# Attention stage of a diffusion trunk: maxima of 512, 256, 768 and 1024 columns, two buffers of turned probabilities, squares in PSUM, roots ahead of the last copy

## The chip, the core and the metric

The kernel runs on one core of one Trainium2 chip. TensorE multiplies matrices into PSUM, VectorE (DVE) and ScalarE (ACT) work elementwise and reduce, GpSimd (POOL) and SyncE (SP) issue transfers. The engines run side by side, each in the order of its own instructions, and wait for one another by semaphores. The metric is the device time of one execution in microseconds; lower is better.

## The reference

One layer of a hybrid trunk over 1024 latent tokens with 256 context tokens ahead of them: differential attention, a convolution branch and a gated delta network, merged, then a mixture of experts. The change lies in the attention alone:

```
def diff_softmax_attend(q, k, v, lam):
    s = jnp.einsum("bhmqd,bhmkd->bhmqk", q, k, preferred_element_type=jnp.float32) * (A_HEAD_DIM ** -0.5)
    p = jax.nn.softmax(s, axis=-1)
    a = p[:, :, 0] - lam * p[:, :, 1]
    return jnp.einsum("bhqk,bhkd->bhqd", a.astype(v.dtype), v)

    def finish(o):
        return (rms_norm(o, subln_w, SUBLN_EPS) * (1.0 - lambda_init)).reshape(o.shape[0], o.shape[1], A_WIDTH)
```

There are 4 heads, each with two maps m of 64 dimensions, 1024 queries in blocks of 128, 1280 keys (256 context, 1024 latent), and values of 128 dimensions. All is fp32.

## The kernel before

The stages run one after the other with a barrier between them; `attend` is one, `branches` follows it. `attend` treats 32 heads of query blocks, numbered j = 4 x block + head. TOK is 1280, P is 128, N is 32, NKT is 10.

For each j these steps are taken. **Scores** (L806, TensorE): six matmuls put both maps' 128 x 1280 scores into the five PSUM banks of `p_scores`; map 0 lies in columns 0 to 1279, map 1 in 1280 to 2559. Their order is map 1 columns 0 to 255, map 0 0 to 511, map 1 256 to 767, map 0 1024 to 1279 ("scored_tails"), map 0 512 to 1023 ("scored0"), map 1 768 to 1279 ("scored1"); the two maps use different halves of the array's rows and run side by side. **Maxima** (L941 to L954, VectorE): the reductions below give each row's maximum of each map, and two "bounds" (L946) turn them into the exponentials' bias `minus_max`. **Exponentials** (L885, ScalarE): one per map over 1280 columns, with the sum. **Sums and mix** (L967, L968, L974, VectorE): the ratio of the sums, and p0 + ratio x p1 into `p0`. **Turn** (L821, TensorE): ten transposes in three groups, of 4, 4 and 2, into two PSUM buffers `p_turned`. **Store** (L872, ScalarE): the three groups are copied to `aT` in SBUF. **Weigh** (L830, TensorE): ten matmuls of `aT` with the values into `p_out`. **Save** (L898, L899, ScalarE): the sum of the squares of the output, with the squares themselves written to `o_squares`, which nobody reads, and the scaled output to `o_raw`. **Root** (L905, ScalarE), for a batch of 8 heads or 4, five times (after heads 7, 15, 23, 27 and 31): the square root needs another function table than the exponential, so a table is loaded (ACT_TABLE_LOAD) ahead of it and another ahead of the next exponential. **Norm** (L982, L983, VectorE) divides, and L840 and L910 turn and store the finished outputs of a block, in eight of the steps.

The order on each engine is written by hand and software-pipelined. In iteration j TensorE runs scores of j+1, turn of j-2's last group, (finished outputs,) weigh of j-2, turn of j-1's first two groups. ScalarE runs store of j-2's groups 0 and 1, save of j-3, store of j-2's group 2, (finished outputs, root,) exponentials of j+1. VectorE runs sums of j, maxima of j+1, mix of j, (norm). The scores of j+1 wait for both exponentials of j ("exped"), as `p_scores` is one buffer. On VectorE each reduction waits for the one before it (`ch.run` is an instruction and the wait for its own end), and `after(eng, name, j, ...)` waits for step j's signal.

## Time and profile before

| | us |
|---|---|
| median of 3 runs | 2865.71 (2860.67 to 2866.39) |
| the profiled execution, its own time | 2864.54 |
| its span in the trace | 2862.7 |
| attention: first scores start | 958.49 |
| attention: last output copy starts | 1213.12 |

Over the whole span TensorE is busy 90%, VectorE 44%, ScalarE 20%. These are averages over stages with different limits. Attention is about 9% of the span, and what a change in it is worth is read from its own steps: a repeating pattern of instructions on three engines, in which the end of one engine's wait is another's work. In a row of the trace in order of time the first number is the start in us from the span's start, the second the duration; a bracket tells how long the engine sat idle before it and who released it. The matmul rows of one block are merged, with their count.

### The profile page before, as it was taken

To read this page: it belongs to the slowest core of one execution; us is meant where nothing else is said; L and a number is where in the kernel's file an instruction comes from. 1 tells how busy PE (TensorE), PEld (TensorE's weight loads), DVE (VectorE), ACT (ScalarE), POOL (GpSimd) and SP (SyncE) were. 2 spreads that over 40 slices of the span, in tenths; PEclk is the share of its full clock that TensorE was granted. 3 is DMA by queue.
4 is the path that set the end of the run, shared out by engine and by line. 5 is a ranking of instruction groups with operands and counts; after the bars stand their busy time and mean duration, and the time that the engine had idled before them with its cause. 6 is when DMAs were issued, how large, how long until landed. Compare 5 with 4: busy or idle time off the path is not lost. (4 is left out here: it accounts for less than half of the span.)

```text
span 2862.7 us, 57067 instructions
## 1 busy us (share of the span) xinstructions
PE 2588.4 (90%) x23169; PEld 1366.0 (48%) x23169; DVE 1261.7 (44%) x2179; ACT 568.6 (20%) x1080; POOL 474.1 (17%) x711
## 2 busy tenths in 40 slices
PE   5999858888898788799999999999499999999995
PEld 3444447776444466644444444445244444333442
DVE  2466656664764488504884211125422222222221
ACT  4333222322221377600000110013100000000000
POOL 0011145552111000000000000000023332233222
PEclk7999968999999999999999999999699999999998
DMA  6011010000010000030222231112677899869532
GB/s 236 22 30 36 1 47 11 19 19 31 22 44 0 15 1 1 1 81 26 81 74 77 73 100 59 34 52 95 236 295 268 336 377 400 331 226 352 202 85 77
DMA packets 198512, 320.17 MB, mean 112 GB/s; under 512 B 13601, under 2 KB 135944, under 8 KB 198120
## 3 DMA queue, kind: packets, MB, share of 16 engines
q1 hardware_dynamic: 183175, 294.11, 28.3%
q0 software_dynamic: 15168, 23.60, 3.7%
q8 instruction: 132, 2.16, 0.3%
q14 instruction: 37, 0.30, 0.0%
HBM read 299.63 MB, written 22.50 MB: 113 GB/s over the span
## 5 line engine op out<-in xcount | busy, mean ns | idle before, releaser
L2697 PE MATMUL p_gate_up<-w_unit,rowsT 128*32 128x512 f32 x4672 | 521.7, 597 | 17.6 <-DVEq L2739 8.1
L2034 PE MATMUL p_gate<-hT,w_gate 128*128 128x512 f32 x768 | 341.9, 598 | 6.5 <-DVE region L2158 5.3
L2697 PEld LDWEIGHTS p_gate_up<-w_unit,rowsT 128*32 128x32 f32 x4672 | 162.9, 111 | 331.1 <-issue 304.5
L2711 PE MATMUL p_y<-w_unit,hiddenT 128*32 128x256 f32 x4672 | 268.0, 381 | 1.2 <-DVE hiddenT L2753 1.2
L1080 PE MATMUL p_w<-hT,w_c 128*128 128x512 f32 (+1 forms) x640 | 248.7, 550 | 0.0
L2583 DVE STREAM_TRANSPOSE rows_turned<-rows 128x256 f32<-128x256 f32 x74 | 33.0, 445 | 452.3 <-PE p_gate_up L2697 447.5
L2034 PEld LDWEIGHTS p_gate<-hT,w_gate 128*128 128x128 f32 x768 | 144.0, 191 | 182.3 <-issue 180.7
L2711 PEld LDWEIGHTS p_y<-w_unit,hiddenT 128*32 128x32 f32 x4672 | 163.2, 111 | 123.7 <-issue 44.6
L1080 PEld LDWEIGHTS p_w<-hT,w_c 128*128 128x128 f32 x640 | 121.5, 190 | 124.9 <-issue 121.6
L2734 ACT ACTIVATE sigmoid<-p_gate_up 128x256 f32<-128x256 f32 x73 | 28.2, 386 | 746.0 <-PE p_gate_up L2697 746.0
L2183 DVE SCALAR_TENSOR_TENSOR region<-gated,taps,region x120 | 154.1, 1284 | 16.0
L2664 POOL DMA_INDIRECT sum_rows<-y,rows_to_add x73 | 117.6, 1611 | 150.7 <-DVE y L2761 144.0
L1996 POOL DMA_DIRECT2D half_region<-in_w_out x1 | 1.1, 1102 | 814.8 <-PE p_branch L2039 814.8
L2158 DVE TENSOR_TENSOR product<-p_branch,gate 128x512 f32<-128x512 f32 x32 | 22.1, 691 | 226.9 <-PE p_branch L2039 226.3
L941 DVE TENSOR_REDUCE part_max<-p_scores 128x1 f32<-128x512 f32 (+2 forms) x128 | 105.6, 825 | 36.2 <-PE p_scores L806 30.4
L806 PE MATMUL p_scores<-region 64*128 64x512 f32 (+1 forms) x384 | 84.3, 575 | 26.3 <-ACT p L885 24.8
L2098 ACT ACTIVATE gate<-p_gate 128x512 f32<-128x512 f32 x48 | 28.6, 596 | 358.4 <-PE p_gate L2034 358.4
L830 PE MATMUL p_out<-region,aT 128*128 128x128 f32 x640 | 80.9, 282 | 13.0 <-ACT aT L872 12.7
L885 ACT ACTIVATE p<-p_scores,minus_max 128x1280 f32<-128x1280 f32 x64 | 84.9, 1327 | 26.3 <-DVE minus_max L946 25.8
L1221 DVE SCALAR_TENSOR_TENSOR conv<-raw,head_taps,conv 128x1284 f32<-128x1284 f32 (+1 forms) x48 | 89.0, 1854 | 1.7
L674 DVE RECIPROCAL rinv<-root 128x512 f32<-128x512 f32 (+1 forms) x20 | 60.5, 3025 | 63.2 <-ACT root L609 63.2
L2574 POOL DMA_INDIRECT rows<-xn_rows,rows_to_gather x75 | 74.8, 997 | 62.7 <-POOL rows_to_gather L2652 60.1
(368 smaller groups left out, 3528.3 us busy)
## 6 DMA issues: line engine op xcount, KB each, us to landing
w_unit<-in_w_gate SPq DMA_DIRECT2D x128, 512.0 KB, 14.9
w_unit<-in_w_up SPq DMA_DIRECT2D x128, 512.0 KB, 16.5
w_unit<-in_w_down SPq DMA_DIRECT2D x128, 512.0 KB, 11.7
w_b<-in_w_mod SPq DMA_DIRECT2D x32, 512.0 KB, 3.9
w_gate<-in_w_in SPq DMA_DIRECT2D x24, 512.0 KB
region<-in_w_mod SPq DMA_DIRECT2D x4, 2048.0 KB, 14.7
w_c<-in_w_in SPq DMA_DIRECT2D x16, 512.0 KB
w_branch<-in_w_branch SPq DMA_DIRECT2D x24, 256.0 KB, 4.1
```

The source lines that it names most:

```text
L806: mm = nc.tensor.matmul(score(m, at, size), k.qT[rows, h, q * P:q * P + P], k.kT[rows, h, at:at + size], start=True, stop=True)
L830: last = nc.tensor.matmul(p_o[:, 0:P], aT[:, t * P:(t + 1) * P], k.v[:, t, h * P:(h + 1) * P], start=(t == 0), stop=(t == NKT - 1))
L885: nc.scalar.activation(pm[m][j % (3 - m)][:, :], score(m, 0, TOK), ACT.Exp, bias=nb[:, 2 * (j % 2) + m:2 * (j % 2) + m + 1], scale=SCALE, ...
L941: ch.run(nc.vector.tensor_reduce(to, ap, AX.X, ALU.max))
L1080: last = nc.tensor.matmul(p_w[i % 5][:, 0:size], w[n][:, c, :], k.hT[:, c, at:at + size], start=(c == 0), stop=(c == KD - 1))
L1221: ins = nc.vector.scalar_tensor_tensor(dst, src[:, t:t + size], taps(n)[:, t:t + 1], dst, ALU.mult, ALU.add)
L2034: last = nc.tensor.matmul(p_g[half][:, :], wg[i][:, c, :], k.hT[:, c, CTX + at:CTX + at + 512], start=(c == 0), stop=(c == KD - 1))
L2183: ins = nc.vector.scalar_tensor_tensor(o, shifted(t), taps[:, t:t + 1], o, ALU.mult, ALU.add)
L2574: k.nc.gpsimd.indirect_dma_start(k.xg[:, :], None, k.dram["xn"].rearrange("t (i n) -> (t i) n", i=4), bass.IndirectOffsetOnAxis(ap=k.row_x ...
L2664: nc.gpsimd.indirect_dma_start(quarters("sums"), bass.IndirectOffsetOnAxis(ap=row_y[:, 0:1], axis=0), y[:, :], None, compute_op=ALU.add).t ...
L2697: last = nc.tensor.matmul(p_gu[part, :].rearrange("p (m c r) -> p m c r", m=2, r=BLK), xT[:, c, :], unit[:, :, j], start=(c == 0), stop=(c ...
L2711: last = nc.tensor.matmul(p_y[part, 0:W], hT[:, c, :], k.ring[u % UNITS][:, c % 2, W * j:W * j + W], start=(c == 0), stop=(c == KD - 1))
```

## The change

In `maxima`, the four reductions take other columns. Before: map 0's first 512; both maps' remaining pieces in columns 1024 to 1535 of `p_scores` as two times 256 in one instruction; map 0's columns 512 to 1023; map 1's last 1024; and L953 joins two partial maxima of map 0, so that each bound can take the larger of two. After: map 0's first 512, map 1's first 256, map 0's last 768, map 1's last 1024, each into a cell of `part_max` of its own; the bound takes the larger of two cells. Two waits for bounds go, one for the bound of the head before comes ahead of the first reduction. `aT` becomes two buffers, used in turn, and the copy of group 0 waits for the weighing of head j-2, not j-1. The squares are written to the unused second quarter of `p_out`'s bank. The root moves from behind the copy of group 2 (and the finished outputs) to ahead of it.

```
-        aT = k.sb(st, "aT", [P, NKT * P])
+        aT = [k.sb(st, f"aT{i}", [P, NKT * P]) for i in range(2)]
...
-                        last = nc.tensor.matmul(p_o[:, 0:P], aT[:, t * P:(t + 1) * P],
+                        last = nc.tensor.matmul(p_o[:, 0:P], aT[j % 2][:, t * P:(t + 1) * P],
...
                     if g == 0:
-                        after(act, "attended", j - 1)
-                    nc.scalar.activation(aT[:, at * P:(at + size) * P], p_t[g % 2][:, 0:size * P], ACT.Copy) \
+                        after(act, "attended", j - 2)
+                    nc.scalar.activation(aT[j % 2][:, at * P:(at + size) * P], p_t[g % 2][:, 0:size * P], ACT.Copy) \
...
-                    nc.scalar.activation(osq[:, :], p_o[:, 0:P], ACT.Square, scale=first, accum_out=ssum[:, n:n + 1])
+                    nc.scalar.activation(p_o[:, P:2 * P], p_o[:, 0:P], ACT.Square, scale=first,
+                                         accum_out=ssum[:, n:n + 1])
...
                     if whole(j - 3):
                         save(j - 3)
+                    for i, qs in enumerate(BATCHES):
+                        if j - 3 == HEADS * qs[-1] + HEADS - 1:
+                            take_root(i)
                     if whole(j - 2):
                         store(j - 2, 2)
                     if outputs_in(j) is not None:
                         store_outputs(outputs_in(j))
-                    for i, qs in enumerate(BATCHES):
-                        if j - 3 == HEADS * qs[-1] + HEADS - 1:
-                            take_root(i)
...
-                        nc.vector.tensor_scalar(nb[:, n:n + 1], part[:, 3:4], part[:, m:m + 1], -SCALE, ALU.max,
-                                                ALU.mult).then_inc(s("maxed"), 1)
-
+                        nc.vector.tensor_scalar(nb[:, n:n + 1], part[:, 2 * m:2 * m + 1], part[:, 2 * m + 1:2 * m + 2],
+                                                -SCALE, ALU.max, ALU.mult).then_inc(s("maxed"), 1)
+
+                    after(dve, "maxed", j - 1, 2, 1)
                     after(dve, "scored_first", j)
-                    reduce(part[:, 2:3], score(0, 0, 512))
+                    reduce(part[:, 0:1], score(0, 0, 512))
                     after(dve, "scored_tails", j)
-                    reduce(part[:, 0:2], p_s[:, 1024:1536].rearrange("p (m n) -> p m n", m=2))
-                    ch.run(nc.vector.tensor_tensor(part[:, 0:1], part[:, 0:1], part[:, 2:3], ALU.max))
+                    reduce(part[:, 2:3], score(1, 0, 256))
                     after(dve, "scored0", j)
-                    reduce(part[:, 3:4], score(0, 512, 512))
+                    reduce(part[:, 1:2], score(0, 512, 768))
                     bound(0)
                     after(dve, "scored1", j)
-                    after(dve, "maxed", j, 2, 0)
                     reduce(part[:, 3:4], score(1, 256, 1024))
                     bound(1)
-                    after(dve, "maxed", j, 2, 1)
```

VectorE, one step of the stage, before. The rows of sums come first, then the maxima, then the mix.

```order
L968 SCALAR_TENSOR_TENSOR sum_ratio<-inverse_sum,rows,exp_sum 128x1
L941 TENSOR_REDUCE part_max<-p_scores 128x1
L941 TENSOR_REDUCE part_max<-p_scores 128x2
L953 TENSOR_TENSOR part_max<-part_max 128x1
L941 TENSOR_REDUCE part_max<-p_scores 128x1
L946 TENSOR_SCALAR minus_max<-part_max 128x1
L941 TENSOR_REDUCE part_max<-p_scores 128x1
L946 TENSOR_SCALAR minus_max<-part_max 128x1
L974 SCALAR_TENSOR_TENSOR p_149<-p_152,sum_ratio,p_149 128x1280
```

The same step of VectorE after the change; x3 are the reductions of 512, 256 and 768 columns.

```order
L966 SCALAR_TENSOR_TENSOR sum_ratio<-inverse_sum,rows,exp_sum 128x1
L941 TENSOR_REDUCE part_max<-p_scores 128x1 x3
L946 TENSOR_SCALAR minus_max<-part_max 128x1
L941 TENSOR_REDUCE part_max<-p_scores 128x1
L946 TENSOR_SCALAR minus_max<-part_max 128x1
L972 SCALAR_TENSOR_TENSOR p_149<-p_152,sum_ratio,p_149 128x1280
```

The join of two maxima is gone, and three reductions stand ahead of the first bound as before.

ScalarE, the step of the first root (iteration 10), before: from the save of head 7 to the exponentials of head 11.

```order
L898 ACTIVATE o_squares,o_square_sum<-p_out,inverse_sum 128x128
L899 ACTIVATE o_raw<-p_out,inverse_sum 128x128
L872 ACTIVATE aT<-p_turned_167 128x256
L905 ACT_TABLE_LOAD
L905 ACTIVATE o_root<-o_square_sum,eps 128x8
L885 ACT_TABLE_LOAD
L885 ACTIVATE p_150,exp_sum<-p_scores,minus_max 128x1280
L885 ACTIVATE p_152,exp_sum<-p_scores,minus_max 128x1280
```

The same place after the change.

```order
L897 ACTIVATE p_out,o_square_sum<-p_out,inverse_sum 128x128
L899 ACTIVATE o_raw<-p_out,inverse_sum 128x128
L905 ACT_TABLE_LOAD
L905 ACTIVATE o_root<-o_square_sum,eps 128x8
L871 ACTIVATE aT_153<-p_turned_167 128x256
L884 ACT_TABLE_LOAD
L884 ACTIVATE p_150,exp_sum<-p_scores,minus_max 128x1280
L884 ACTIVATE p_152,exp_sum<-p_scores,minus_max 128x1280
```

The first load and the root moved ahead of the copy of group 2, and the second load stays with the exponential. The number of loads is the same.

## Rows read from the trace of the kernel before

**Rows 1.** Page, costliest groups: busy, mean ns | idle before, releaser.
```profile
L806 PE MATMUL p_scores<-region 64*128 64x512 f32 (+1 forms) x384 | 84.3, 575 | 26.3 <-ACT p L885 24.8
```

**Rows 2.** Order of time: start, duration, engine, line; fourth and 32nd block of scores.
```profile
983.67 2.42 PE L806 MATMUL p_scores<-region 64*128 64x256 f32 x12 [3.11 <-ACT p L885]
...
1184.37 2.42 PE L806 MATMUL p_scores<-region 64*128 64x256 f32 x12 [0.20 <-ACT p L885]
```

**Rows 3.** Order of time, one plain step.
```profile
1061.18 2.42 PE L806 MATMUL p_scores<-region 64*128 64x256 f32 x12 [0.21 <-ACT p L885]
...
1062.33 0.38 ACT L899 ACTIVATE o_raw<-p_out,inverse_sum 128x128 f32<-128x128 f32 x1
1062.35 1.42 DVE L941 TENSOR_REDUCE part_max<-p_scores 128x1 f32<-128x512 f32 x2 [0.76 <-PE p_scores L806]
...
1063.80 0.16 DVE L953 TENSOR_TENSOR part_max<-part_max 128x1 f32<-128x1 f32 x1
1063.99 0.69 DVE L941 TENSOR_REDUCE part_max<-p_scores 128x1 f32<-128x512 f32 x1
1064.01 0.38 ACT L872 ACTIVATE aT<-p_turned 128x256 f32<-128x256 f32 x1 [1.29 <-PE p_turned L821]
...
1064.44 2.50 PE L830 MATMUL p_out<-region,aT 128*128 128x128 f32 x20 [0.47 <-ACT aT L872]
1064.72 0.21 DVE L946 TENSOR_SCALAR minus_max<-part_max 128x1 f32<-128x1 f32 x1
1064.97 1.33 ACT L885 ACTIVATE p<-p_scores,minus_max 128x1280 f32<-128x1280 f32 x1 [0.58 <-DVE minus_max L946]
1065.04 1.22 DVE L941 TENSOR_REDUCE part_max<-p_scores 128x1 f32<-128x1024 f32 x1
...
1066.30 0.21 DVE L946 TENSOR_SCALAR minus_max<-part_max 128x1 f32<-128x1 f32 x1
1066.55 1.33 ACT L885 ACTIVATE p<-p_scores,minus_max 128x1280 f32<-128x1280 f32 x1 [0.16 <-DVE minus_max L946]
...
1066.78 1.04 PE L821 MATMUL p_turned<-const,p 128*128 128x128 f32 x8
...
1068.02 2.42 PE L806 MATMUL p_scores<-region 64*128 64x256 f32 x12 [0.20 <-ACT p L885]
```

**Rows 4.** Order of time, the step of the first root.
```profile
1038.59 2.42 PE L806 MATMUL p_scores<-region 64*128 64x256 f32 x12 [0.20 <-ACT p L885]
...
1041.42 0.38 ACT L872 ACTIVATE aT<-p_turned 128x256 f32<-128x256 f32 x1 [1.29 <-PE p_turned L821]
1041.82 1.28 ACT L905 ACT_TABLE_LOAD   x1
...
1043.11 0.30 ACT L905 ACTIVATE o_root<-o_square_sum,eps 128x8 f32<-128x8 f32 x1
1043.43 1.28 ACT L885 ACT_TABLE_LOAD   x1
...
1044.73 1.33 ACT L885 ACTIVATE p<-p_scores,minus_max 128x1280 f32<-128x1280 f32 x1
...
1046.05 1.32 ACT L885 ACTIVATE p<-p_scores,minus_max 128x1280 f32<-128x1280 f32 x1
...
1047.51 2.42 PE L806 MATMUL p_scores<-region 64*128 64x256 f32 x12 [2.28 <-ACT p L885]
```

**Rows 5.** Order of time, the step behind the second root.
```profile
1104.26 3.87 PE L806 MATMUL p_scores<-region 64*128 64x256 f32 x12 [2.28 <-ACT p L885]
...
1108.24 0.69 DVE L941 TENSOR_REDUCE part_max<-p_scores 128x1 f32<-128x512 f32 x1 [0.81 <-PE p_scores L806]
...
1112.52 2.42 PE L806 MATMUL p_scores<-region 64*128 64x256 f32 x12
```

**Rows 6.** Lines by form, the attention stage: busy, mean ns | idle before.
```profile
L941 DVE TENSOR_REDUCE part_max<-p_scores 128x1 f32<-128x512 f32 x64 | 44.3, 692 | 30.6 <-PE p_scores L806 29.4 <-DVE part_max L953 0.3
L941 DVE TENSOR_REDUCE part_max<-p_scores 128x1 f32<-128x1024 f32 x32 | 39.2, 1224 | 3.7 <-DVE minus_max L946 0.5
```

**Rows 7.** Order of time, the weighing behind the fourth root.
```profile
1195.18 3.44 PE L830 MATMUL p_out<-region,aT 128*128 128x128 f32 x20
```

More of the change, by code:

```diff
@@ L750, in attend @@
         o_n = k.sb(st, "o_normed", [P, 2 * HEADS, P])
-        osq = k.sb(st, "o_squares", [P, P])
         ssum = k.sb(st, "o_square_sum", [P, 4 * HEADS])
```

## Prediction

> **What bounds the kernel now.** I looked first at the page, to see which engine the stage waits on, then at the order of time of one attention step, and last at the steps that differ from it. The reader is to see in the page's row of the score matmuls that TensorE sits idle 26.3 us before them and that ScalarE, with the exponentials of the step before, releases nearly all of it [rows 1]. Attention is 32 steps (8 query blocks times 4 heads). In step j TensorE computes the scores of head j+1 while everything else works on heads j to j-3, so the score matmuls mark the steps. The time from their fourth start, 983.67, to their 32nd, 1184.37 [rows 2], is 28 steps, 200.70 us: 23 plain ones of 6.84, 3 with a root of 8.92 and 2 right behind them of 8.26, and that adds up (157.3 + 26.8 + 16.5).
>
> A plain step is one closed chain [rows 3], counted from the start of the scores at 1061.18. VectorE's first maximum begins at +1.17, the small maximum of maxima (L953) at +2.62, the third reduction at +2.81, the first bound at +3.54, the reduction of 1024 columns at +3.86, the second bound at +5.12, ScalarE's second exponential at +5.37, and the next scores at +6.84. Every piece is busy time plus 0.03 to 0.25 of hand-over, so **the maxima on VectorE are the path**, not TensorE. TensorE's own round is shorter: the eight transposes start at +5.60 and take 1.04, so it could start the next scores at +6.64. It has 0.20 to spare. ScalarE has a hole of 1.30: its copy of the output ends at 1062.71 and the copy of the last turned group begins at 1064.01.
>
> **The change part by part.**
>
> *Maxima.* The reductions fit a line: 0.692 us for 512 columns, 1.224 for 1024 [rows 6], so 0.16 + 0.53 per 512 columns. My estimates from it are 0.43 for 256 and 0.96 for 768. Now there are 512, 256, 768, 1024: the same 2560 columns in four reductions, and L953 is gone. The first still starts at +1.17, the 256 one at +1.90 (0.73 behind, as now), and VectorE would be free for the 768 one at +2.36. But that one needs the fifth score matmul, which runs beside the sixth. The block ends at +2.42, and where VectorE does wait for it, at the lower clock, it starts 0.11 after the block's end (1108.24 against 1104.26 + 3.87) [rows 5]. So it starts at +2.46 to +2.53, not at +2.36: **part of the gain turns into a wait for TensorE.** The first bound follows at +3.46 to +3.53 instead of +3.54. Behind it the wait for its own signal goes: bound to reduction is now 0.32, bound plus a normal gap is 0.21 + 0.04, so 0.07 less. Together a plain step gains 0.08 to 0.15; I take 0.11. The upper bound is the whole 0.19 + 0.07 = 0.26, but TensorE's 6.64 caps it at 0.20. The lower bound is zero if the 256 reduction costs as much as one of 512 (0.69): the 768 one would then start at +2.63 and the bound come at +3.63, which the 0.07 nearly pays back. The second bound and the exponential just move. The price is a loss at the lower clock: there the fifth matmul comes at +3.98, and 768 columns behind it instead of 512 take 0.27 longer, less 0.07: a low step gets 0.20 longer.
> Plain steps: the 23 and the first one, 24 x 0.11 = **2.6 us**. The waits for "maxed" that move to the head of the next maxima are met long before.
>
> *Two buffers of turned probabilities.* The copy of group 0 waited for the weighting of head j-1. TensorE weighs head j-1 ahead of turning head j, so the wait for the turn, which stays, already implies it. **Nothing**, and nothing is late next.
>
> *Squares into PSUM.* The Square of 128 columns and its readout lie ahead of the hole of 1.30. A cost or a gain of 0.1 each is swallowed there; it shows only in the steps with a root and in the last three heads, 7 places. No row shows ScalarE writing PSUM. The nearest price is the same Square now, 0.38; I take zero and keep -0.1 to +0.1 each, 0.7 either way.
>
> *Roots.* Five of them; the last has no exponentials behind it and gains nothing. A root now takes table load 1.28, root 0.30, table load 1.28 between the last copy and the exponentials [rows 4]: the copy starts at 1041.42 and the first exponential at 1044.73, 3.31 later, against 0.96 in a plain step. The step is 8.92 (1038.59 to 1047.51), 2.08 more than 6.84. Afterwards load and root go behind the copy of the output. That copy ends at 1.53 after the scores (1040.12), the load runs to 1041.42 and the root to about 1041.73, so of 1.58 us the hole covers 1.30 and the third copy starts 0.2 to 0.3 late, ending at 1042.03 to 1042.13. Queued behind it on ScalarE are the second load and the exponentials; TensorE waits for the copy with the weighting, which starts 0.2 to 0.3 late, and that leaves its transposes ready at +6.9 to +7.0, ahead of the new step's end. The second load then runs to 1043.4, the first exponential starts there, the second 1.32 later (1044.73 to 1046.05 in the row) and the scores 1.46 after that: 1046.1 to 1046.2. VectorE's second bound is ready by 1043.9 and does not bind. A root step becomes 7.5 to 7.65, 1.3 less. Three in the steps and the fourth in front of the tail: 4 x 1.3 = **5.2 us**. VectorE's division and multiplication for the root stay behind its mix and end before its next maximum.
>
> The Trainium skill, "ScalarE: Activation LUTs", section "What ACT_TABLE_LOAD costs", gives 1283 ns for the load, as the row has it, and adds a drain of some 1380 ns for every switch of table. This trace disagrees on the second: the load starts 0.02 after the copy before it ends, and two loads and a root take 2.9 us in all. With the page's drain in both loads of the new order a root step would take 10.4 and the roots would lose 6 us instead of gaining 5.2.
>
> *Clock.* Behind two of the three roots in the steps TensorE fell from 2.4 to 1.2 GHz: it had idled 2.28 us, then the scores took 3.87 instead of 2.42 and the step 8.26 [rows 5]. Behind the fourth root the weighting took 3.44 instead of 2.50 [rows 7]. With the roots moved the idle time ahead of the scores is 0.6 to 0.7, close to the 0.20 of plain steps where no fall is seen, plus 0.3 more ahead of the weighting. I take it that these falls go: 2 x 1.42 + 0.94 = **3.8 us**. Bounds: zero, and those 3.8. The two low steps at the stage's start stay and lose 2 x 0.20 = 0.4.
>
> **Sum**: 2.6 + 5.2 + 3.8 - 0.4 = 11.2 us. The profiled execution took 2864.5 and would take 2853.3; the median of the runs is 1.2 above it, so **2854.5**. The stages behind attention start at a barrier and just move.
>
> **The rivals.**
> 1. *The falls of the clock stay.* For: TensorE still waits longer in a root step than in a plain one (0.8 for the copy, 0.6 ahead of the scores). Against: both gaps together are less than the 2.28 + 0.47 of now. Without the 3.8, and with 3 x 0.2 lost on the low steps that stay: 2858.9.
> 2. *The maxima gain nothing*: the wait for the fifth matmul eats L953's time, or the short reduction costs more than the line. For: the 0.10 to 0.17 of wait worked out above. Against: the 0.07 after the bound is independent of it. 2854.5 + 2.6 = 2857.1; with rival 1 on top 2861.5.
> 3. *Slower: TensorE spends more of the stage at 1.2 GHz.* Place: the weighting in a root step, which now waits for a copy behind load and root. Each low step costs 1.42, plus 0.20 for the longer third maximum. Roots and maxima still gain 7.4, so this decides from 5 low steps more than now, and from 9 it is over 0.2% slower. If each of the three root steps leaves four low ones, 12 instead of 2, it is 10 x 1.62 - 7.4 = 8.8 more: 2874.5. Against: the first root's step, with the 2.28 us gap, fell not at all, and the others recovered within one step.
> 4. *The table switch costs more in its new place*, because ScalarE has just written PSUM and results in flight must settle. If each load costs one load's length more (1.28 twice, 4 roots) the roots lose 5.0 instead of gaining 5.2; with the clock falling as now the sum is 2.6 - 5.0 - 0.4 - 0.6, so 2869. The roots turn to a loss from 0.65 us per load, the whole from 0.85. Against: the gap of 0.02 in front of loads. The page named above stands for this case.
> 5. *The change does less than it says*: only the order of the root matters, the rest is none. That is rival 2.
>
> **How the numbers follow.** The forecast 50%, rival 1 alone 18%, rival 2 alone 14%, both 8%, rival 3 4%, rival 4 2%, and 4% for something I don't see, half of it over 0.2% slower. Rival 4's 2869 is within 0.2%. A measurement tells 0.2%, 5.7 us, from no change, so faster means under 2860.0. The forecast and rival 2 alone lie there nearly whole, rival 1 in 15 of its 18, both together hardly: 50 + 12 + 15, so 77% faster; 17% the same; 6% slower. The range runs from 2849 (steps capped at 0.20 gain, 2.2 more, squares 0.7 faster, the starting falls gone too) to 2861.5 (rivals 1 and 2 together).
>
> **What would show it.** Steps between scores: 6.70 to 6.76 in plain ones. VectorE idle just ahead of the 768 reduction, by TensorE. The reductions 0.43 and 0.96 long. Bound to reduction 0.25. In a root step the load at 0.02 behind the output's copy, ScalarE's hole gone, the third copy 0.2 to 0.3 late, the step 7.5 to 7.65. Score blocks all 2.42 long behind the roots. I am wrong if a plain step stays at 6.84, if a root step is over 8.3, or if score blocks of nearly 4 us stand behind the roots.

## The result, and the profile after

| | before | after |
|---|---|---|
| median of 11 runs each | 2865.36 (2858.91 to 2878.43) | 2847.49 (2839.33 to 2854.69) |
| ratio of the times | | 0.9938, 95% interval 0.9922 to 0.9954 |
| the profiled execution: its time, its span | 2864.54, 2862.7 | 2846.19, 2843.9 |
| attention, first scores to the next stage's first matmul | 257.19 | 241.63 |
| a plain step | 6.84 | 6.62 |
| a root step | 8.92 | 7.50 |
| score blocks near 4 us behind a root | 2 | 0 |

The kernel got 17.9 us faster; 11.2 were forecast, and 2847.5 lies below the range's 2849. Of the 18.8 us between the two spans 15.6 lie in attention. The rest lies in code that the change doesn't touch: ahead of attention 1.0 more, behind it 4.2 less. Both parts scatter like that without any change, as the repeats below show: there the changed kernel has 7.1 more ahead of attention and 1.8 more behind it. So **15.6 us is what is to be explained**, against 11.2.

The page's row of the score matmuls, which answers [rows 1] (busy, mean ns | idle before, releaser):

```profile
L805 PE MATMUL p_scores<-region 64*128 64x512 f32 (+1 forms) x384 | 81.3, 558 | 16.3 <-ACT p L884 14.8
```

TensorE's idle time ahead of scores fell from 26.3 to 16.3 us, and their mean from 575 to 558 ns, as the two score blocks that took nearly 4 us behind a root take 2.42 now. Order of time in the kernel after, one plain step, to be read beside [rows 3] (start, duration, engine, line; bracket: idle before, releaser):

```profile
1030.81 2.42 PE L805 MATMUL p_scores<-region 64*128 64x256 f32 x12
...
1032.05 2.25 DVE L941 TENSOR_REDUCE part_max<-p_scores 128x1 f32<-128x512 f32 x3 [0.83 <-PE p_scores L805]
...
1033.63 0.38 ACT L871 ACTIVATE aT<-p_turned 128x256 f32<-128x256 f32 x1 [1.30 <-PE p_turned L820]
...
1034.33 0.21 DVE L946 TENSOR_SCALAR minus_max<-part_max 128x1 f32<-128x1 f32 x1
1034.46 1.21 DVE L941 TENSOR_REDUCE part_max<-p_scores 128x1 f32<-128x1024 f32 x1
...
1035.96 1.33 ACT L884 ACTIVATE p<-p_scores,minus_max 128x1280 f32<-128x1280 f32 x1
...
1036.41 1.04 PE L820 MATMUL p_turned<-const,p 128*128 128x128 f32 x8
1037.43 2.42 PE L805 MATMUL p_scores<-region 64*128 64x256 f32 x12
```

The first bound starts at +3.52 (before +3.54), so the columns alone gave next to nothing. The 1024 reduction starts 0.13 behind the bound's start (before 0.32): there lies the gain. The profile also shows no idle time ahead of the scores any more. Still, it is the second exponential that releases them: they start 1.47 behind its start, as before (1066.55 to 1068.02 in [rows 3], 1035.96 to 1037.43 here). The reductions by form (busy, mean ns | idle before) are as estimated from the line through [rows 6], 0.43 and 0.96:

```profile
L941 DVE TENSOR_REDUCE part_max<-p_scores 128x1 f32<-128x768 f32 x32 | 30.6, 957 | 6.6 <-PE p_scores L805 2.7
...
L941 DVE TENSOR_REDUCE part_max<-p_scores 128x1 f32<-128x256 f32 x32 | 13.6, 424 | 1.4 <-PE p_scores L805 0.3
```

The step of the first root, after, beside [rows 4]:

```profile
1038.57 0.39 ACT L899 ACTIVATE o_raw<-p_out,inverse_sum 128x128 f32<-128x128 f32 x1
...
1038.97 1.28 ACT L905 ACT_TABLE_LOAD   x1
...
1040.27 0.30 ACT L905 ACTIVATE o_root<-o_square_sum,eps 128x8 f32<-128x8 f32 x1
1040.48 0.36 ACT L871 ACTIVATE aT<-p_turned 128x256 f32<-128x256 f32 x1
1040.86 1.28 ACT L884 ACT_TABLE_LOAD   x1
...
1042.15 1.33 ACT L884 ACTIVATE p<-p_scores,minus_max 128x1280 f32<-128x1280 f32 x1
...
1044.93 2.42 PE L805 MATMUL p_scores<-region 64*128 64x256 f32 x12 [0.67 <-ACT p L884]
```

ScalarE has no hole left: copy, load, root, copy, load and exponential follow one another. TensorE's gap ahead of the scores is 0.67 instead of 2.28. TensorE's rows that answer [rows 2] and [rows 7]: the fourth and the 32nd block of scores, and the weighing behind the fourth root:

```profile
984.48 2.42 PE L805 MATMUL p_scores<-region 64*128 64x256 f32 x12 [3.18 <-ACT p L884]
...
1172.46 2.42 PE L805 MATMUL p_scores<-region 64*128 64x256 f32 x12
...
1181.82 2.50 PE L829 MATMUL p_out<-region,aT 128*128 128x128 f32 x20 [0.20 <-ACT aT L871]
```

The 28 steps take 187.98 us instead of 200.70: 25 of 6.62 and 3 of 7.50. The weighing takes 2.50 instead of 3.44. Windows of the kernel after (window and length, then busy us and count of PE, PE's loads, DVE, ACT, POOL, then the granted clock, DMA share, GB/s) show the granted clock at 1.00 all through this stretch, which leaves out the low-clock steps at the stage's start; the same window of the kernel before had 0.98:

```profile
990.00:1180.00 190.00, 175.86 (x1211) 136.80 (x1209) 158.95 (x262) 148.22 (x301) 0.00 (x0) 1.00 0.00 1
```

### The profile page after: what moved, and what is told of

It is laid out like the page before. It is cut to its first block and busy times, and to the rows that moved or that the text cites. A ratio compares the mean times of both kernels' runs of the same rounds, so it can differ in the third digit from the quotient of the medians.

```text
span 2843.9 us, 57001 instructions
## 1 busy us (share of the span) xinstructions
PE 2572.6 (90%) x23169; PEld 1341.7 (47%) x23169; DVE 1250.2 (44%) x2147; ACT 566.2 (20%) x1080; POOL 472.6 (17%) x711
## 5 line engine op out<-in xcount | busy, mean ns | idle before, releaser
L2695 PEld LDWEIGHTS p_gate_up<-w_unit,rowsT 128*32 128x32 f32 x4672 | 153.7, 111 | 338.6 <-issue 311.9
L2709 PEld LDWEIGHTS p_y<-w_unit,hiddenT 128*32 128x32 f32 x4672 | 154.4, 110 | 131.5 <-issue 44.5
L941 DVE TENSOR_REDUCE part_max<-p_scores 128x1 f32<-128x512 f32 (+3 forms) x128 | 105.2, 822 | 35.3 <-PE p_scores L805 30.3
L805 PE MATMUL p_scores<-region 64*128 64x512 f32 (+1 forms) x384 | 81.3, 558 | 16.3 <-ACT p L884 14.8
```

The source lines that it names most:

```text
L805: mm = nc.tensor.matmul(score(m, at, size), k.qT[rows, h, q * P:q * P + P], k.kT[rows, h, at:at + size], start=True, stop=True)
L941: ch.run(nc.vector.tensor_reduce(to, ap, AX.X, ALU.max))
L2695: last = nc.tensor.matmul(p_gu[part, :].rearrange("p (m c r) -> p m c r", m=2, r=BLK), xT[:, c, :], unit[:, :, j], start=(c == 0), stop=(c ...
L2709: last = nc.tensor.matmul(p_y[part, 0:W], hT[:, c, :], k.ring[u % UNITS][:, c % 2, W * j:W * j + W], start=(c == 0), stop=(c == KD - 1))
```

## The experiments

In each, the time of attention is the measure, from the first scores to the next stage's first matmul; two profiles of one kernel agree in it within 0.1 us. The whole program's medians are given where a kernel was timed in rounds; the kernels without one were run once, and only their traces count. In the last two rows a score block begins before the second exponential is done, so their root's cost falls on two steps, and the blocks of 3.59 there are stretched by that wait, at full clock.

| kernel | attention | plain step | root step | long score blocks (3.4 to 4.2 us) behind a root | median, ratio to before (95%) |
|---|---|---|---|---|---|
| before | 257.19 | 6.84 | 8.92 | 2 | |
| roots alone | 249.23 | 6.84 | 7.51 | 0 | 2854.09, 0.9965 (0.9944 to 0.9986) |
| maxima alone | 250.29 | 6.62 | 8.92 | 1 | 2858.38, 0.9978 (0.9965 to 0.9992) |
| waits alone | 253.56 | 6.71 | 8.91 | 2 | |
| columns alone | 256.91 | 6.82 | 8.91 | 2 | |
| after, one buffer, squares in SBUF | 241.54 | 6.62 | 7.50 | 0 | 2855.25, 0.9963 (0.9948 to 0.9978) |
| after, 256 reduction left out | 243.10 | 6.65 | 7.50 | 0 | |
| after, transposes earlier | 240.89 | 6.62 | 7.50 | 0 | 2848.25, 0.9935 (0.9912 to 0.9958) |
| and map 0's scores first | 252.78 | 6.92 | 7.73, then 7.35 | 0 | 2860.58, 0.9978 (0.9966 to 0.9990) |
| and head start, map 0's second piece third | 239.85 | 6.13 and 6.83, mean 6.48 | 7.74 and 7.04 or 6.83 before it | 0 | 2846.32, 0.9928 (0.9916 to 0.9941) |

### Roots alone, maxima alone

The kernel before with only the root's loop moved:

```
                     if whole(j - 3):
                         save(j - 3)
+                    for i, qs in enumerate(BATCHES):
+                        if j - 3 == HEADS * qs[-1] + HEADS - 1:
+                            take_root(i)
                     if whole(j - 2):
                         store(j - 2, 2)
                     if outputs_in(j) is not None:
                         store_outputs(outputs_in(j))
-                    for i, qs in enumerate(BATCHES):
-                        if j - 3 == HEADS * qs[-1] + HEADS - 1:
-                            take_root(i)
```

> The kernel before with the root moved ahead of the copy of group 2, nothing else. Theory: the moved root gives two things by itself, a root step of 7.6 to 7.7 us instead of 8.92 (the changed kernel's 7.50 had shorter maxima and a Square that is 0.03 shorter) and no score block of nearly 4 us behind the roots. Plain steps stay 6.84. Attention, from the first scores to the first matmul of the next stage, falls from 257.2 to 246 to 248 us. Rival (the clock's falls hang on something else): root steps of 7.6 but score blocks of 3.9 us stay behind one or two of the three roots, attention 249 to 251 us.

The kernel before with only the changed maxima (four reductions, cells, bounds and waits, as in the change):

```
-                    reduce(part[:, 0:2], p_s[:, 1024:1536].rearrange("p (m n) -> p m n", m=2))
-                    ch.run(nc.vector.tensor_tensor(part[:, 0:1], part[:, 0:1], part[:, 2:3], ALU.max))
+                    reduce(part[:, 2:3], score(1, 0, 256))
...
-                    reduce(part[:, 3:4], score(0, 512, 512))
+                    reduce(part[:, 1:2], score(0, 512, 768))
```

> The kernel before with the new maxima and their waits, nothing else. Theory: plain steps 6.62 us as in the changed kernel, root steps 8.7 to 8.9, score blocks of nearly 4 us behind some roots as before; attention falls by 5 to 7 us from 257.2. Rival (the plain step needs the two buffers or the squares in PSUM too): plain steps 6.65 to 6.75.

Measured: the roots alone took 8.0 us off attention, the maxima alone 6.9. Together that is 14.9 of the 15.6. Order of time with the roots alone, the first root's step: the scores at its start and at its end; last, the weighing that began at 1195.42, in the tail:

```profile
1047.36 2.42 PE L806 MATMUL p_scores<-region 64*128 64x256 f32 x12 [0.20 <-ACT p L885]
...
1054.87 2.42 PE L806 MATMUL p_scores<-region 64*128 64x256 f32 x12 [0.67 <-ACT p L885]
...
1195.42 4.12 PE L830 MATMUL p_out<-region,aT 128*128 128x128 f32 x20 [0.21 <-ACT aT L872]
```

The root step is 7.51, as long with the old maxima as the 7.50 with the new ones, and no score block behind a root is long. One trace with three roots can't show that the falls are gone, for with the maxima alone one of the two was missing too, behind the same 2.28 us of idle time. All traces together can: where the root stands in its old place (before, its repeat, maxima alone, waits alone, columns alone) TensorE idles 2.28 us in all 15 places, and the block behind took 3.48 to 4.11 instead of 2.42 in 9 of them (with the granted clock at 0.50, as from 1105.1 to 1108.4 in the kernel before); where it was moved, TensorE idles 0.67 (18 places in six traces) or 1.10 (3, transposes earlier), and no block is long. So **moving the root is what removes the long score blocks**.

That the two parts give 14.9 together and not 15.6 is the balance of two larger differences. From the fourth to the 32nd score block they give 7.1 and 6.9, that is 1.2 more than the 12.7 of the whole change, since the fall that was missing with the maxima alone is counted twice. In the tail they give 0.8 and -0.1, that is 2.0 less than the 2.7 of the whole. There, with the roots alone, one weighing took 4.12 instead of 2.50 (granted clock 0.50 from 1195.7 to 1199.0), after waits of TensorE of 0.68, 1.16 and 0.21; after the whole change it took 2.50 behind 0.67, 1.16 and 0.20, and so it did in the five other kernels with moved roots and these steps, while it took 3.37 to 3.64 in all five with the root in its old place. Why it ran low with the roots alone, no run here settles.

### Waits alone, columns alone

The step of 6.62 was 0.11 shorter than the 6.73 of the forecast, so the maxima were cut in two. The old columns, with the map 1 maximum in a cell of its own, so that the waits for the bounds can go:

```
-                        nc.vector.tensor_scalar(nb[:, n:n + 1], part[:, 3:4], part[:, m:m + 1], -SCALE, ALU.max,
+                        nc.vector.tensor_scalar(nb[:, n:n + 1], part[:, 3 + m:4 + m], part[:, m:m + 1], -SCALE, ALU.max,
...
+                    after(dve, "maxed", j - 1, 2, 1)
                     after(dve, "scored_first", j)
...
-                    after(dve, "maxed", j, 2, 0)
-                    reduce(part[:, 3:4], score(1, 256, 1024))
+                    reduce(part[:, 4:5], score(1, 256, 1024))
                     bound(1)
-                    after(dve, "maxed", j, 2, 1)
```

> The kernel before with the old columns and the join of maxima, but the two waits for the bounds' own signals taken out (each bound reads cells of its own) and the one at the head of the next maxima put in. Theory A: what shortened the plain step is the wait behind the bound, 0.19 us and not the 0.07 of the prediction. Then bound to reduction of 1024 is 0.13 us here and the step is 6.65 to 6.72. Rival B: the gain came from the columns; then this step is 6.77 or more.

And the new columns with the old waits:

```
-                    after(dve, "maxed", j - 1, 2, 1)
...
+                    after(dve, "maxed", j, 2, 0)
                     reduce(part[:, 3:4], score(1, 256, 1024))
                     bound(1)
+                    after(dve, "maxed", j, 2, 1)
```

(shown against the change's maxima).

> The kernel before with the new columns (512, 256, 768, 1024, no join), but the waits for the bounds' own signals kept as before. Theory A: the first bound comes at 3.46 to 3.54 us after the scores' start as the 768 reduction waits for TensorE, so the step is 6.76 to 6.84. Rival B: step 6.65 to 6.70.

Order of time, waits alone:

```profile
1016.91 2.42 PE L806 MATMUL p_scores<-region 64*128 64x256 f32 x12
...
1018.14 1.42 DVE L941 TENSOR_REDUCE part_max<-p_scores 128x1 f32<-128x512 f32 x2 [0.83 <-PE p_scores L806]
...
1020.51 0.21 DVE L946 TENSOR_SCALAR minus_max<-part_max 128x1 f32<-128x1 f32 x1
1020.64 1.22 DVE L941 TENSOR_REDUCE part_max<-p_scores 128x1 f32<-128x1024 f32 x1
...
1023.62 2.42 PE L806 MATMUL p_scores<-region 64*128 64x256 f32 x12
```

Order of time, columns alone:

```profile
1011.87 2.42 PE L806 MATMUL p_scores<-region 64*128 64x256 f32 x12 [0.18 <-ACT p L885]
...
1013.04 1.15 DVE L941 TENSOR_REDUCE part_max<-p_scores 128x1 f32<-128x512 f32 x2 [0.76 <-PE p_scores L806]
...
1014.39 0.96 DVE L941 TENSOR_REDUCE part_max<-p_scores 128x1 f32<-128x768 f32 x1 [0.21 <-PE p_scores L806]
...
1015.39 0.21 DVE L946 TENSOR_SCALAR minus_max<-part_max 128x1 f32<-128x1 f32 x1
...
1015.71 1.23 DVE L941 TENSOR_REDUCE part_max<-p_scores 128x1 f32<-128x1024 f32 x1
...
1018.68 2.42 PE L806 MATMUL p_scores<-region 64*128 64x256 f32 x12 [0.18 <-ACT p L885]
```

**The waits are worth 0.13, the columns 0.02.** Without the wait the 1024 reduction starts 0.13 behind the bound's start, that is 0.08 before the bound ends; with it, 0.32. The difference is 0.19, not the 0.07 of the forecast. Of it 0.06 is lost again at the head, where the first reduction now has two waits and starts at +1.23 instead of +1.17. With the columns alone L953's time turns into the predicted wait: VectorE sits idle 0.21 for the fifth score matmul, the 768 reduction starts at +2.52 and the bound at +3.52. The two together give 0.22, more than 0.02 + 0.13, because the 0.06 of the later head then falls into that wait of 0.21 and costs nothing: 0.02 + 0.19 = 0.21, and 0.22 was measured.

Not every wait for the instruction before costs 0.19. In the old step the third reduction also waits for the end of the one before it, and starts only 0.03 behind that end ([rows 3]: 1063.80 + 0.16 to 1063.99); behind the bound it is 0.11 (1064.72 + 0.21 to 1065.04). The trace's own records show the difference: where an instruction waits for more than one semaphore, an EVENT_SEMAPHORE of 0.02 us stands ahead of it in VectorE's instructions and waits for one of them. For the third reduction that was the score matmul's, long since given; ahead of the 1024 reduction it was the bound's own signal, and its record starts at 1064.97, behind the bound's end at 1064.94. So the 0.19 are two parts: 0.12 for waiting for the predecessor's end at all (from 0.08 ahead of it to 0.03 behind it), and 0.07 for having that wait in an instruction of its own. The 0.06 at the head is of the second kind: with two waits, the one for the score matmul, which comes last, has gone into the EVENT_SEMAPHORE.

The Trainium skill, "VectorE: DVE Perf Modes", section "The DRAIN you can't avoid", holds that a semaphore after each of a row of VectorE instructions costs nothing extra, and its table of rules says to minimise instructions, not semaphores. This case's traces disagree on the semaphore, behind a bound of 0.21 us: the wait taken out was worth 0.19 us in every step, 0.12 of it for any wait on the predecessor. They don't speak against taking out instructions: L953's 0.19 of VectorE's time did go, but TensorE's fifth matmul came last there, so that only 0.02 was left of it.

### What holds the step at 6.62

The 256 reduction left out; map 1's bound then takes the larger of its own 1024 columns and map 0's last 768 (the expectation says map 0's first part, which the edit doesn't do):

```
-                        nc.vector.tensor_scalar(nb[:, n:n + 1], part[:, 2 * m:2 * m + 1], part[:, 2 * m + 1:2 * m + 2],
+                        nc.vector.tensor_scalar(nb[:, n:n + 1], part[:, m:m + 1], part[:, 2 * m + 1:2 * m + 2],
...
                     after(dve, "scored_tails", j)
-                    reduce(part[:, 2:3], score(1, 0, 256))
                     after(dve, "scored0", j)
```

> The changed kernel with the reduction of map 1's first 256 columns left out (its maximum is over the other 1024 and map 0's first part). VectorE's chain gets shorter only as far as TensorE lets it: the 768 reduction then starts at 2.47 us after the scores, the bound at 3.45. Theory: TensorE's own round of 6.62 binds now, with no idle time left ahead of the scores, so the step stays 6.62. Rival: VectorE and ScalarE still bind; the step falls to 6.55.

```profile
1012.44 2.42 PE L805 MATMUL p_scores<-region 64*128 64x256 f32 x12
...
1015.00 0.96 DVE L941 TENSOR_REDUCE part_max<-p_scores 128x1 f32<-128x768 f32 x1 [0.63 <-PE p_scores L805]
...
1015.99 0.21 DVE L946 TENSOR_SCALAR minus_max<-part_max 128x1 f32<-128x1 f32 x1
...
1019.09 2.42 PE L805 MATMUL p_scores<-region 64*128 64x256 f32 x12
```

With 0.42 us less work VectorE just waits longer (0.63), the bound comes at +3.55, and the step is 6.65. Neither expectation held, as neither had a loss in it. The loss is again a wait: `after(dve, "scored_tails", j)` stays, so the 768 reduction now has three semaphores to wait for. By the trace's records it starts 0.12 behind the fifth matmul's signal here (1014.875 to 1014.997), and 0.09 behind it in the changed kernel (1033.244 to 1033.337). **TensorE's fifth matmul sets the first bound**, and VectorE's work ahead of it is free.

The other side: transposes of group 0 taken ahead of the weighing (in steps without finished outputs), which the second `aT` buffer and a swap of the `p_turned` buffers allow, so that fewer stand between VectorE's mix and the scores:

```
+                    if whole(j - 1) and q is None:
+                        turn(j - 1, 0)
                     if whole(j - 2):
...
-                        last = nc.tensor.transpose(p_t[g % 2][:, t * P:(t + 1) * P],
+                        last = nc.tensor.transpose(p_t[(j + g) % 2][:, t * P:(t + 1) * P],
```

> The changed kernel, TensorE's work in another order: the turn of the next head's group 0 goes between the turn of group 2 and the weighing, in steps without finished outputs, where TensorE waits 0.47 us for ScalarE's copy; the two PSUM buffers are taken in turn over all groups for it. TensorE's round falls to about 6.15 us. Theory: VectorE's chain ties with TensorE at 6.62, so the step stays 6.60 to 6.62 and TensorE idles 0.3 to 0.5 ahead of the scores. Rival (only TensorE binds): the step falls to 6.5 or less.

```profile
1013.55 2.42 PE L805 MATMUL p_scores<-region 64*128 64x256 f32 x12 [0.42 <-ACT p L886]
...
1020.17 2.42 PE L805 MATMUL p_scores<-region 64*128 64x256 f32 x12 [0.42 <-ACT p L886]
```

TensorE now sits idle 0.42 ahead of the scores, and the step is still 6.62. So what binds is the loop scores, fifth matmul, bounds, exponentials, scores, and an earlier turn alone gains nothing in a plain step. TensorE's own round is close behind it, but doesn't tie. In the changed kernel the scores start 0.26 behind the start of the last transpose and 0.045 behind the signal of the second exponential, in every plain step; where nothing holds TensorE, in the two kernels of the next part, they start 0.20 behind that transpose. By these rows TensorE has some 0.06 to spare. My estimate is therefore that faster maxima behind the bound would gain no more than 0.06 a step unless the turn comes earlier too; no run tried it. The 0.7 us of this kernel come from the tail (27.95 instead of 28.66).

### Scores with a head start

The loop can only be cut where it closes, at the scores' wait for both exponentials. Map 0's scores need only map 0's exponential, 1.4 us earlier. First with map 0's two pieces ahead of map 1's:

```
-                    after(pe, "exped", j - 1, 2, 1)
+                    after(pe, "exped", j - 1, 2, 0)
...
-                    for m, at, size, name in ((1, 0, 256, "scored_low"), (0, 0, 512, "scored_first"), (1, 256, 512, None),
-                                              (0, 1024, 256, "scored_tails"), (0, 512, 512, "scored0"),
+                    for m, at, size, name in ((0, 0, 512, "scored_first"), (0, 512, 512, "scored0"), (1, 0, 256, "scored_low"),
+                                              (1, 256, 512, None), (0, 1024, 256, "scored_tails"),
                                               (1, 768, 512, "scored1")):
+                        if (m, at) == (1, 0):
+                            after(pe, "exped", j - 1, 2, 1)
```

> The kernel e7_order with the scores of map 0, columns 0 to 1023, ahead of map 1's, waiting for the first exponential of the head before instead of the second. Theory: both ties are loosened, TensorE starts map 0 before the second exponential is done, VectorE's first maximum comes 0.4 us earlier against it; steps of 6.35 to 6.5 in the 17 or so plain steps without outputs and up to 6.6 with them, attention 4 to 7 us shorter than the changed kernel's 241.6. Rival: the tails of map 0 wait for map 1's first piece, the reductions of 256 and 768 come later and the step stays 6.6 or grows.

```profile
1015.29 3.21 PE L807 MATMUL p_scores<-region 64*128 64x512 f32 x12
...
1017.37 0.30 PEld L807 LDWEIGHTS p_scores<-region 64*128 64x128 f32 x4 [0.84 <-PE p_scores L807]
...
1018.17 1.42 DVE L945 TENSOR_REDUCE part_max<-p_scores 128x1 f32<-128x256 f32 x2 [0.96 <-PE p_scores L807]
...
1022.21 3.21 PE L807 MATMUL p_scores<-region 64*128 64x512 f32 x12
```

My theory fell and the rival held as it was put: the tails of map 0 wait for map 1's first piece. The block takes 3.21 instead of 2.42, and the step 6.92. The tails share a PSUM bank with that piece, so the kernel has them wait for its signal, "scored_low". In the old order that piece is the first one; here it stands behind map 0's second piece. The row of PEld, TensorE's weight loads, shows the wait: the loads of the last two pieces come 0.84 behind the others, held by a score matmul, where the kernel before has all twelve loads of a block in one run:

```profile
1061.18 1.59 PEld L806 LDWEIGHTS p_scores<-region 64*128 64x128 f32 x12 [0.44 <-ACT p L885]
```

By the trace's records "scored_low" was signalled at 1017.324, 0.04 behind map 0's second piece (1017.282), though the record of map 1's first piece ends at 1016.50: the signals came in the order of the program. So the last two pieces begin 2.08 into the block, and 1.40 into it in the old order.

The wait isn't the whole of it. This kernel's very first block waits for no exponential and takes 3.18. In its records map 1's first piece starts 0.01 behind map 0's, so the two halves of the array do run side by side here too. But map 1's last piece stands behind the tails in the order and starts 0.01 behind them; until then its half has nothing to do, while map 0's half is busy with two long pieces in a row. Each piece is two matmuls there, and those of 512 columns follow one another at 0.43 on a half. Map 0's second piece has its last one at 963.95, so the tails could begin at 964.37, and they begin at 964.63. My estimate from these starts is that of the 0.76 more than 2.42 the wait is 0.26 and the order 0.50.

Then with map 1's first piece second: map 0's 512, map 1's 256, map 0's 512, map 1's 512, then the tails and map 1's last piece, and the maxima in that order. The first line is shown against the kernel just above, the reductions against the changed kernel; each bound reads the cells that belong to it:

```
-                    for m, at, size, name in ((0, 0, 512, "scored_first"), (0, 512, 512, "scored0"), (1, 0, 256, "scored_low"),
+                    for m, at, size, name in ((0, 0, 512, "scored_first"), (1, 0, 256, "scored_low"), (0, 512, 512, "scored0"),
...
-                    reduce(part[:, 0:1], score(0, 0, 512))
+                    reduce(part[:, 5:6], score(0, 0, 512))
                     after(dve, "scored0", j)
+                    reduce(part[:, 6:7], score(0, 512, 512))
+                    ch.run(nc.vector.tensor_tensor(part[:, 0:1], part[:, 5:6], part[:, 6:7], ALU.max))
+                    after(dve, "scored_tails", j)
+                    reduce(part[:, 1:4:2], p_s[:, 1024:1536].rearrange("p (m n) -> p m n", m=2))
```

> The kernel e7_order with map 0's first piece ahead of map 1's, waiting for the first exponential only, then map 0's second piece, and the tails fifth; the maxima are 512, 512, join, two times 256, 1024. TensorE's slack of 0.42 us becomes a head start for map 0, whose columns are complete 0.2 to 0.3 us earlier against the second exponential. Theory: the wait for map 0's scores is what holds the first bound, so plain steps fall to 6.35 to 6.5, attention to 235 to 238 us. Rival (TensorE's row halves don't overlap in this order, as in e8_early): the block of scores grows over 3 us and the step is 6.6 or more.

```profile
1017.59 2.42 PE L807 MATMUL p_scores<-region 64*128 64x512 f32 x12
...
1023.72 3.12 PE L807 MATMUL p_scores<-region 64*128 64x512 f32 x12
```

Attention took 239.85, the least of all, but 2 us more than I had expected at most. The steps alternate, 6.13 and then 6.83 (further on 6.34 and 6.62), 6.48 in the mean, which is inside the 6.35 to 6.5 of the expectation: a block that starts early stretches to 3.12, since its map 1 pieces still wait for the second exponential, and gives the lead back in its own step, to the next block. What the expectation lacked is the roots: the two steps at a root take 14.56 to 14.78 together, where the changed kernel takes 6.62 + 7.50 = 14.12. The median of 2846.32 is lower than the change's, yet its interval overlaps the change's own, so only the trace of the stage tells that it is better.

### Buffers and squares, and the repeats

The change without the second buffer and with the squares in SBUF:

```
-        aT = [k.sb(st, f"aT{i}", [P, NKT * P]) for i in range(2)]
+        aT = [k.sb(st, "aT", [P, NKT * P])] * 2
...
-                        after(act, "attended", j - 2)
+                        after(act, "attended", j - 1)
...
-                    nc.scalar.activation(p_o[:, P:2 * P], p_o[:, 0:P], ACT.Square, scale=first,
+                    nc.scalar.activation(osq[:, :], p_o[:, 0:P], ACT.Square, scale=first,
```

> The changed kernel with one buffer aT again and the squares back in SBUF. Theory: neither does anything for the time. Plain steps 6.62, root steps 7.50 to 7.53 (the Square is 0.03 longer in front of the table load), the last heads' steps 4.99 to 5.02, attention 241.6 to 242 us. Rival: the second buffer lets the copy start earlier, then the step is longer than 6.65 here.

Attention took 241.54 us against 241.63: nothing. But the whole program came to 2855.25, ratio 0.9963 (0.9948 to 0.9978), where the change had 0.9938. The intervals barely overlap, and no step of attention differs. So before, after and this kernel were run again, together and in 5 rounds:

> The kernel before, unchanged, as a kernel of its own. What two readings of one program differ by: the ratio is 1.000 within 0.2%, attention takes 257 us, and the part ahead of attention, which was 958.5 us in the first trace and 959.5 to 967.4 in the others with the same code there, shows how much of a whole-program difference is not attention's.

> The changed kernel, unchanged, once more. Theory: the change is worth what attention shows, 15.6 us (257.2 to 241.6), and the rest of the 17.9 between the medians is scatter of the other stages; here the gain is then 13 to 18 us and attention 241.5. Rival: the changed kernel has a further 2 to 3 us elsewhere; then the part ahead of attention or behind it is shorter than in the kernel before in this trace too.

> The changed kernel with one buffer aT and the squares in SBUF again. Its attention took 241.5 us as the changed kernel's, but its median was 7.8 us above. Theory: scatter between sets of runs; here it is within 4 us of the changed kernel's second reading. Rival: where the tiles lie in SBUF matters to other stages; then it is 6 to 10 us above it again.

| kernel, again | attention | median | ratio to before (95%) |
|---|---|---|---|
| before | 257.27 | 2865.50 | 1.0003 (0.9992 to 1.0013) |
| after | 241.53 | 2852.61 | 0.9950 (0.9937 to 0.9963) |
| after, one buffer, squares in SBUF | 241.59 | 2849.99 | 0.9941 (0.9927 to 0.9954) |

This time the order is reversed. **Both edits are worth nothing**, and the medians of a kernel that isn't touched in this respect move by some 5 us from one set of runs to the next, about as much as one interval reaches to either side. The repeats ran on another chip than the first experiments, so whether the set or the chip moves them stays open. The traces show where it happens: in whatever kernel, attention's start lies between 958.5 and 971.9 us and what follows attention takes 1641.0 to 1647.0, while attention itself repeats to 0.1.

## Why the prediction was right or wrong

The sum forecast 11.2 us; attention gave 15.6. By the steps of the trace:

| term | forecast | measured |
|---|---|---|
| plain steps | 24 x 0.11 = 2.6 | 157.4 to 152.2 for 23: 5.2 |
| roots in the steps | 3 x 1.3 = 3.9 | 8.92 to 7.50: 3 x 1.41 = 4.2 |
| the low steps behind them | 2 x 1.42 = 2.8 | 16.52 to 13.24: 3.3 |
| tail, with the fourth root | 1.3 + 0.94 = 2.2 | 31.31 to 28.66: 2.65 |
| start of the stage, two low steps | -0.4 | 25.18 to 24.99: +0.2 |

(The forecast's 24 steps hold the first one, which stands in the last row of the measured.)

**The step that failed is the term of the plain steps**, and in it "bound plus a normal gap is 0.21 + 0.04, so 0.07 less". The mechanism was right, and its size wrong by a factor of nearly three: 0.19. The normal gap was read from instructions of which each waits for the end of the one before ([rows 3]: 1062.35 + 1.42 to 1063.80). The 0.07 is right for what it was read from: it is the price of having that wait in an instruction of its own. But no wait for the bound was left at all, and an instruction whose waits are all met starts before its predecessor ends, by 0.08, as the rows of the waits alone show; that is the other 0.12. The plain steps are 2.6 of the missing 4.4 us. (In the kernel before 22 of the 23 take 6.83 and one takes 7.08, with 0.44 of idle time ahead of the scores; all take 6.62 after, and this one step is 0.25 of the 2.6.) The two low steps behind roots are another 0.4 (they became steps of 6.62, not 6.84). The root steps owe nothing to it, as they take 7.51 with the old maxima: there the forecast took 7.62 out of its own 7.5 to 7.65, and 0.3 is missing. The start is 0.6 of the rest and the tail 0.4.

At the start the sign was wrong. Its reason was right, as the second low step shows, in order of time from the first reduction on, before and then after:

```profile
977.64 0.69 DVE L941 TENSOR_REDUCE part_max<-p_scores 128x1 f32<-128x512 f32 x1 [1.70 <-PE p_scores L806]
...
980.38 0.21 DVE L946 TENSOR_SCALAR minus_max<-part_max 128x1 f32<-128x1 f32 x1
...
980.69 1.23 DVE L941 TENSOR_REDUCE part_max<-p_scores 128x1 f32<-128x1024 f32 x1
```

```profile
978.39 0.69 DVE L941 TENSOR_REDUCE part_max<-p_scores 128x1 f32<-128x512 f32 x1 [1.78 <-PE p_scores L805]
...
981.38 0.21 DVE L946 TENSOR_SCALAR minus_max<-part_max 128x1 f32<-128x1 f32 x1
981.51 1.21 DVE L941 TENSOR_REDUCE part_max<-p_scores 128x1 f32<-128x1024 f32 x1
```

The bound comes 0.25 later behind the first reduction (2.99 instead of 2.74), the 1024 reduction 0.19 closer behind the bound, and the step takes 8.27 instead of 8.14, a loss of 0.13 as against the forecast 0.20. But the first low step went from 9.13 to 8.83. There VectorE had sat idle 0.47 behind the bound, where it is 0.10 in the other steps:

```profile
972.55 1.22 DVE L941 TENSOR_REDUCE part_max<-p_scores 128x1 f32<-128x1024 f32 x1 [0.47 <-DVE minus_max L946]
```

The repeat of the kernel before and the roots alone have that idle time too, the kernels with the waits or the columns changed don't; where it came from, no run here shows.

**Right, point by point.** The 768 reduction waits for the fifth score matmul and starts at +2.52, inside the forecast 2.46 to 2.53, and the bound at +3.52 in 3.46 to 3.53. The reductions' durations held. The signs that did not come are those of the failed term: plain steps of 6.70 to 6.76 (6.62), and 0.25 from bound to reduction (0.13). TensorE's round was said to cap a step's gain at 0.20. That cap was reckoned from the modelled end of the transposes and is some 0.27 by the starts (they lie 0.47 apart in the kernel before, 0.20 where nothing holds TensorE), so the gain of 0.22 passed it and didn't run into it. The root step at 7.50 lies at the edge of 7.5 to 7.65, with the third copy 0.23 late (at +3.05 of the step, against +2.82 in a plain one). The clock's falls behind roots went; for the score blocks the roots' move alone did it, while one weighing of the tail still ran low with it. The number of long score blocks, two, which the sum took from one trace, had luck in it: over all traces of the old place it is 9 in 15. Two buffers and squares were nothing: the Square does take 350 ns on average instead of 0.38 us, hidden ahead of the hole, as this row of lines by form shows:

```profile
L897 ACT ACTIVATE p_out<-p_out,inverse_sum 128x128 f32<-128x128 f32 x32 | 11.2, 350 | 2.6 <-PE p_out L829 2.6
```

Of the rivals, the second was half true: the columns gained next to nothing (0.02), and what it set against itself, the wait behind the bound, paid for nearly all. Rivals 1, 3 and 4 didn't happen. Against the fourth: the load at 1038.97 starts 0.01 after the copy before it ends, in its new place too, and the Trainium skill's drain of some 1380 ns at each switch ("ScalarE: Activation LUTs", "What ACT_TABLE_LOAD costs") shows in neither place.

**The range.** By the forecast's own reckoning attention's 15.6 us would give 2865.7 - 15.6 = 2850.1, inside the range by 1.1. That, too, is luck: the lower end of 2849 counts the falls at the stage's start as gone, which they aren't, and without them it is 2854.5 - 2.2 - 0.7 = 2851.6, and attention's 15.6 us alone would have left the range. What put the median below 2849 is the rest of the program, which the range had no allowance for: in the first set the medians differ by 17.9, that is 2.3 more than attention, and in the repeats by 2865.5 - 2852.6 = 12.9, that is 2.7 less. So two errors are to be told apart: attention's gain of 4.4 us more than the sum, most of it the mis-sized term, and a scatter of 2 to 3 us, which the range lacked.

## What to carry to other kernels

Take a gap between two instructions on one engine from a pair that stands in the same relation as the new pair will: a gap behind a wait for the predecessor's own end says nothing on what remains when that wait goes. In a loop of several engines look for short instructions that wait for one another through semaphores before cutting work out; here giving a result a cell of its own, so that a wait could go, was worth 0.19 us behind the bound in every step (0.13 of the step where nothing else was changed), and the instruction saved 0.02, as another engine came last there. Measure an edit of one stage in that stage's own trace where the rest of the program scatters more than the edit is worth.

## What the runs showed of the hardware

A VectorE instruction whose waits are met starts 0.08 us before its predecessor ends (1020.51 + 0.21 to 1020.64 with the waits alone). A wait for the predecessor's end moves it to 0.03 behind that end, and to 0.11 if that wait sits in an instruction of its own, ahead of it. With more than one semaphore to wait for, such an instruction stands there; where it held the semaphore that came last, the reduction started 0.06 to 0.07 later (+1.23 instead of +1.17 at the head), and with a third semaphore another 0.03. Matmuls on the two halves of the array's rows start 0.01 us apart and run side by side, but TensorE's signals came in the order of the program: a short matmul behind a longer one of the other half was signalled 0.04 us behind that one, 0.83 after the end of its own record. And TensorE's clock behind the same idle time of 2.28 us fell in 9 of 15 root steps, so that a gain which rests on it has to be taken from several steps.
